# Windowed attention of a hybrid layer rebuilt on half-height tiles, with the values product split around the output projection

## The reference, cut to what matters

```python
def block(i):                                  # for 16 blocks of queries
    q0 = i * Q_BLOCK
    qb = lax.dynamic_slice_in_dim(qg, q0, Q_BLOCK, axis=1)      # 8 heads of 64, 2 kv heads
    kb = lax.dynamic_slice_in_dim(k_pad, q0, band, axis=1)      # band = 384 keys
    vb = lax.dynamic_slice_in_dim(v_pad, q0, band, axis=1)
    valid = ((jnp.abs(k_pos[None, :] - q_pos[:, None]) <= WINDOW)
             & (k_pos[None, :] >= 0) & (k_pos[None, :] < seq_len))
    s_band = jnp.where(valid, einsum(qb, kb) * ATT_SCALE, NEG_INF)
    s_ctx = einsum(qb, kc) * ATT_SCALE                          # 256 context keys
    p = jax.nn.softmax(jnp.concatenate([s_sink, s_ctx, s_band], axis=-1), axis=-1)
    o = einsum(p[..., 1:1 + n_ctx], vc) + einsum(p[..., 1 + n_ctx:], vb)
mix = jnp.concatenate([rms_norm(att, gw[:ATT_W]), rms_norm(hy, gw[ATT_W:])], axis=-1) @ w_out
x = x + g1 * mix
# router: the best of 4 groups, then the best two of its 8 experts
```

## Time and profile before

| | us |
|---|---|
| runs shown, median (lowest to highest) | 2907.66 (2897.3 to 2910.91) |
| the profiled execution | 2909.62 |
| its span, first to last instruction | 2907.9 |
| granted TensorE clock, mean over the span | 0.916 |
| stage 5, first scores to the start of stage 6 | 758.1 |
| PE busy / VectorE / ScalarE / GpSimd over the span | 2491.6 / 1310.2 / 1101.7 / 727.6 |

### The profile page before, as it was taken

One profiled execution on the slowest core, in us unless ns is written; L12 is line 12 of the kernel. 1 busy time (PEld: TensorE's weight loads), 2 busy tenths in 40 slices (PEclk: granted clock), 3 DMA queues, 4 the chain that ended last, 5 costly groups with the idle time before them and its releaser, 6 DMA issues. The chain is left out here.

```text
span 2907.9 us, 45576 instructions
## 1 busy us (share of the span) xinstructions
PE 2491.6 (86%) x15491; PEld 1681.2 (58%) x15492; DVE 1310.2 (45%) x2225; ACT 1101.7 (38%) x2047; POOL 727.6 (25%) x1383
## 2 busy tenths in 40 slices
PE   4887999999959998699999999608888998777997
PEld 1334544444436665589988888505555665544664
DVE  4535473212215554224455444206544665444663
ACT  2542121111124443224454444106444555344562
POOL 1650010000001110512555555531122122221211
PEclk9998999999969998559999999758998999989998
DMA  4983111211173442401111111028876987674893
GB/s 170 314 254 110 31 44 29 73 44 44 29 201 81 118 97 55 120 15 59 59 58 58 58 53 44 30 95 308 283 234 192 348 304 245 225 226 125 297 323 117
DMA packets 238325, 404.73 MB, mean 139 GB/s; under 512 B 24805, under 2 KB 127725, under 8 KB 233413
## 3 DMA queue, kind: packets, MB, share of 16 engines
q1 hardware_dynamic: 160183, 329.28, 33.7%
q0 software_dynamic: 18416, 44.58, 6.6%
q10 hardware_dynamic: 59616, 29.38, 3.7%
HBM read 336.60 MB, written 74.49 MB: 141 GB/s over the span
## 5 line engine op out<-in xcount | busy, mean ns | idle before, releaser
L799 PE MATMUL ps_proj<-sb_hT,sb_win 128*128 128x512 f32 x768 | 336.1, 597 | 7.6 <-DVE sb_rot L904 6.0
L799 PEld LDWEIGHTS ps_proj<-sb_hT,sb_win 128*128 128x128 f32 x768 | 145.7, 192 | 189.9 <-issue 183.0
L2316 PE MATMUL ps_byp<-sb_w,sb_gT 128*128 128x512 f32 x512 | 237.4, 607 | 3.9 <-ACT sb_gT L2131 3.9
L2042 DVE TENSOR_TENSOR sb_w1l<-sb_raw,sb_w1h 128x1024 fp32r<-128x1024 f32 x128 | 148.2, 1220 | 166.3 <-ACT sb_w1h L2103 166.3
L1811 DVE CUSTOM_DVE_ANT_0 sb_pr<-ps_S,sb_mask 128x640 f32<-128x640 f32 x128 | 105.5, 824 | 216.4 <-PE ps_S L1660 216.3
L1346 POOL TENSOR_TENSOR sb_zr<-sb_zr,sb_skip 128x512 f32<-128x512 f32 x32 | 40.0, 1280 | 608.5 <-DMA sb_skip<-in_hy_skip 458.6
L1739 ACT COPY sb_pt<-ps_PT 128x512 f32<-128x512 f32 x128 | 74.7, 584 | 271.4 <-PE ps_PT L1666 271.3
L1680 PE MATMUL ps_O<-sb_v,sb_pt 128*128 128x64 f32 (+1 forms) x1280 | 172.2, 289 | 0.0
L1680 PEld LDWEIGHTS ps_O<-sb_v,sb_pt 128*128 128x128 f32 x1280 | 169.4, 210 | 0.0
L2316 PEld LDWEIGHTS ps_byp<-sb_w,sb_gT 128*128 128x128 f32 x512 | 93.9, 194 | 99.7 <-issue 93.5
L746 PE MATMUL ps_proj<-sb_hT,sb_win 128*128 128x512 f32 x320 | 143.0, 601 | 9.2 <-DMA sb_win<-in_w_in 8.6
(11 more groups left out here) (298 smaller groups left out, 5485.0 us busy)
## 6 DMA issues: line engine op xcount, KB each, us to landing
sb_raw<-in_exp_w SPq DMA_DIRECT2D x64, 2048.0 KB, 15.3
sb_w<-in_exp_w SPq DMA_DIRECT2D x32, 2048.0 KB, 9.9
sb_ada<-in_ada_w SPq DMA_DIRECT2D x16, 1536.0 KB, 8.4
scr_filt<-sb_fout ACTq DMA_DIRECT2D x128, 128.0 KB, 4.4
sb_yh<-scr_filt SPq DMA_DIRECT2D x64, 256.0 KB, 5.0
sb_win<-in_w_in SPq DMA_DIRECT2D x9, 1024.0 KB, 5.6
sb_xr<-in_x SPq DMA_DIRECT2D x16, 512.0 KB, 5.1
sb_gt<-scr_hy_in SPq DMA_DIRECT2D x8, 1024.0 KB, 7.3
```

The lines of the kernel that those rows point to most:

```text
L799: ins = pe.matmul(mp[:, (NQ + n) % 4, :], w[:, pc % 3, k, (ct % 2) * P:(ct % 2 + 1) * P], g.hT[:, k, c * 512:(c + 1) * 512], start=(k == 0 ...
L2042: ve.tensor_tensor(piece(low[m], part), piece(raw13[par][:, m], part), piece(high[m], part).bitcast(F32), ALU.subtract).then_inc(lo[m], 1)
L2316: ins = pe.matmul(yp[:, part, :], gT[:, f, :], w2[par][:, f, part * 512:(part + 1) * 512], start=(f == 0), stop=(f == FT - 1), skip_group_ ...
```

## The change

Scores: the keys of the band lie in rows 0 to 63 of `g.kT`, those of the context in rows 64 to 127, and the queries are loaded into both halves of the rows, so that a head's scores are two products over 64 rows each. The bias row goes; a mask with three variants (first, inner, last tile) takes its place. The heads are taken in the order 0, 4, 1, 5, 2, 6, 3, 7.

Values: the exponentials of all heads are kept (`pt`, one buffer), transposed in ten chunks of four blocks each, ahead of the scores in `head(p)`. Then the values are the weights (64 columns) and two heads at a time stream past them (256 columns), kv head 0 to partitions 0 to 63 of the result and kv head 1 to 64 to 127. The result lies transposed, is copied by ScalarE (`ot`) and turned back by four transposes (`turn_values`). The first half of the product stands between heads 3 and 4, the second between the projection's two halves, the turn after the second half.

Routing: the picks move from GpSimd to VectorE, in three parts behind heads 0, 1 and 2; GpSimd combines them. The inverse roots of the mixer's norm move from VectorE to GpSimd (two operations). On VectorE the normalising moves behind the residual's first half. The router product moves behind head 7. The splitting of `w_out` moves from GpSimd to ScalarE and VectorE, one eighth per head of step 0. All steps are unrolled.

```diff
-    step(Tile(0, -1), True, False, False, False, False)
...
-    with eng.Fori(1, NT // 2 - 1) as j:
-        for off in (1, 2):
-            step(Tile(j, off), True, True, True, True, True)
...
+    for n in range(-1, NT + 3):
+        step(Tile(0, n), n + 1 < NT, 0 <= n < NT, 0 <= n - 1 < NT, 0 <= n - 2 < NT, 0 <= n - 3)
...
+        order = [4 * (p % 2) + p // 2 for p in range(NH)]
+        turns = [(0, 1), (2,), (3,), (4,), (5, 6), (7,), (8,), (9,)]
...
@@ SP
-                    sp.dma_start(qb[b.par][0:HD, :, :], ...)
+                    for part in (slice(0, HD), slice(HD, 2 * HD)):
+                        sp.dma_start(qb[b.par][part, :, :], ...)
...
@@ GpSimd
+                    pool.wait_ge(rt1, pl.n + 1)
...
+                    pool.tensor_tensor(pick[:, b, 2, :], pick[:, b, 0, :], pick[:, b, 1, :], ALU.add).then_inc(picked, 1)
...
+                if values:
+                    pool.wait_ge(sqa, t.n + 1)
...
+                    do(pool.tensor_scalar(nw[:, 1, :], ms[:, t.par, :], 1.0 / HW, EPS, ALU.mult, ALU.add))
+                    rsqrt(nw[:, 0, :], nw[:, 1, :], 2).then_inc(mxr, 1)
@@ TensorE
+                def head(p):
+                    if values:
+                        for c in turns[p]:
+                            pe.wait_ge(ex, 8 * t.n + (4 * c + 3) // 5 + 1)
+                            if c == 1:
+                                wait(pe, att, t.n)
+                            else:
+                                wait(pe, tc, 10 * t.n + (c - 1 if c else 0))
...
+                        pe.matmul(S[:, 512 - C:512], qb[nx.par][HD:2 * HD, h, :], g.kT[HD:2 * HD, kv, 0:C],
+                                  start=True, stop=True)
+                        pe.matmul(S[:, 512:512 + 3 * P], qb[nx.par][0:HD, h, :],
+                                  g.kT[0:HD, kv, bass.ds(nx.n * P, 3 * P)], start=True, stop=True).then_inc(qk, 1)
+
+                def tile_values(half):
+                    pe.wait_ge(tc, 10 * t.n + 5 * half + 5)
+                    if half == 0:
+                        wait(pe, otc, t.n)
                     for a in range(5):
+                        for kv in range(2):
...
+                            ins = pe.matmul(OT[kv * HD:(kv + 1) * HD, half, :, :], v, x, start=(a == 0), stop=(a == 4),
+                                            skip_group_check=True)
                     ins.then_inc(pv, 1)
+                def turn_values():
+                    pe.wait_ge(otc, t.n + 1)
+                    pe.wait_ge(tc, 10 * t.n + 9)
+                    for a in range(4):
+                        ins = pe.transpose(PT[:, t.par, a * P:(a + 1) * P], ot[:, a, :], g.ident[:, :])
+                    ins.then_inc(ott, 1)
...
+                head(7)
                 if route:
...
-                head(7)
-                if values:
-                    head_values(7)
...
                 if project:
                     pe.wait_ge(t1v, pj.n + 1)
+                    project_half(0)
+                if values:
+                    tile_values(1)
+                if project:
+                    project_half(1)
+                if values:
+                    turn_values()
@@ ScalarE
                 head(7)
+                if values:
+                    act.wait_ge(pv, 2 * t.n + 2)
+                    act.copy(ot[:, :, :]..., OT[:, :, :, :]...).then_inc(otc, 1)
@@ VectorE
                 head(0)
                 if route:
                     residual(ro, 1).then_inc(res, 1)
-                for h in range(1, 4):
-                    head(h)
+                if place:
+                    pick_group()
+                head(1)
+                if place:
+                    pick_first()
+                head(2)
+                if place:
+                    pick_second()
+                head(3)
...
                 if values:
                     ve.wait_ge(eso, t.n + 1)
-                    ve.wait_ge(pv, 8 * t.n + 8)
...
+                    ve.wait_ge(ott, t.n + 1)
+                    ve.tensor_tensor(mix..., PT[:, t.par, :]..., rsum..., ALU.mult).then_inc(att, 1)
...
                 if project:
                     do(residual(pj, 0))
+                if values:
+                    ve.wait_ge(mxr, t.n + 1)
+                    wait(ve, t1, t.n)
+                    ve.tensor_scalar(mixn[:, 0, :], mix[t.par][:, 0, :], nw[:, 0, 0:1], None, ALU.mult)
+                    ve.tensor_scalar(mixn[:, 1, :], mix[t.par][:, 1, :], nw[:, 0, 1:2], None, ALU.mult).then_inc(mxn, 1)
```

More of the change, by code:

```diff
@@ L1487, in stage5 @@
         block = st.enter_context(nc.Block())
[L1489 removed]
+        tables = [(mask[:, :, :], i["mask"].rearrange("p (a k) -> p a k", a=3)), (sink[:, :], i["attn_sink"][0].partition_broadcast(P))]
         later = [
@@ new lines, in turn_values, with project_half @@
+                def turn_values():
+                    pe.wait_ge(otc, t.n + 1)
+                    pe.wait_ge(tc, 10 * t.n + 9)
+                    for a in range(4):
+                        ins = pe.transpose(PT[:, t.par, a * P:(a + 1) * P], ot[:, a, :], g.ident[:, :])
+                    ins.then_inc(ott, 1)
+                def project_half(half):
+                    cs = slice(half * 512, (half + 1) * 512)
+                    for k in range(KT):
+                        pe.matmul(M[:, half, :], mixh[:, k, :], woh[:, k, cs], start=(k == 0), stop=False)
+                        pe.matmul(M[:, half, :], mixh[:, k, :], wol[:, k, cs], start=False, stop=False)
+                        ins = pe.matmul(M[:, half, :], mixl[:, k, :], woh[:, k, cs], start=False, stop=(k == KT - 1))
+                    ins.then_inc(op, 1)
@@ L1686, in step @@
+                for p in range(4):
+                    head(p)
                 if route:
@@ new lines, in head @@
+                        ve.wait_ge(sm, 8 * nx.n + p + 1)
+                        ve.tensor_scalar(nm[:, nx.par, p:p + 1], mx[:, nx.par, p:p + 1], -SCALE,
+                                         nsink[:, order[p]:order[p] + 1], ALU.mult, ALU.min).then_inc(nmx, 1)
+                    if values and isinstance(t.n, int) and t.n == 0:
+                        ve.wait_ge(wo_hi, p + 1)
+                        ve.scalar_tensor_tensor(out=wol[:, p, :], in0=wo[:, p, :], scalar=g.cols[:, C_GN + p:C_GN + p + 1],
+                                                in1=woh[:, p, :].bitcast(F32), op0=ALU.mult, op1=ALU.subtract).then_inc(wo_lo, 1)
```

283 lines of the change are left out of this document (121 added, 162 removed).

## The result

The changed kernel takes 3024.75 us (median of 4 runs, 3023.17 to 3033.76) against 2905.81 us for the kernel before (4 runs beside them): 1.0429 times as long, 95% interval 1.0400 to 1.0458. The prediction was 3013, slower with a chance of 0.92. The profiled execution took 3024.8 us with a span of 3023.0.

A forecast was written before the change was run, and what follows sets the result against it. TensorE was taken to set the pace in the middle of the kernel before. Start -29, middle +146 and tail -12 on the profiled 2909.6 us gave 3015, with the median at 3013; range 2965 to 3060.

The forecast's parts named there:

- TensorE's own work: TensorE's work per tile in the loop: 31.2 us against 37, worth 6 us only if TensorE still set the pace.
- The chain: One walk round a loop step, VectorE and TensorE waiting in turn: 45.8 us a tile, 50.3 with the clock's fall.
- C: Loop step, VectorE's masks, residual's second half, picks (5.1) and xn before TensorE can go on with heads: 11.4 us.
- The clock: TensorE's clock falls in each tile during heads 0 to 3: 4.5 us extra a tile, bounds 0 and about 10.
- D: Loop step, TensorE from xn's hand-over through transposes, values and scores until mask 4: 5.4 us, +3 at half speed.
- A: Loop step, TensorE from first projected half to turned values: 13.9 us, +1.5 for the clock at the projection's start.
- The first rival: The clock stays at 1.00 in the loop, 45.8 us a tile: 2951 us; chance 0.15.
- The second rival: Paired passes in scores and values run one after the other, 8 us a tile more: 3117 us; chance 0.05.
- F: Loop step, round trip of head 5 between TensorE's scores and VectorE's mask: 2.1 us.
- G: Loop step, head 7's scores, router, then VectorE's logits, mask 7 and mixl before the projection may start: 6.1 us.
- The tail: End of stage 5: two GpSimd pick chains of 20.1 us replaced, -26; longer steps +12 and +2: -12 us.
- the third rival: VectorE and TensorE overlap as before, a tile of about 34 us: 2813 us; chance 0.08 with near misses.

The follow-up runs named there:

- two runs: Each against the changed kernel: extra TensorE products after heads 0 to 3 and the router, 2986.50 us; router's bias addition moved behind mixl, 2980.24 us.
- The run in one row group: Changed kernel with context scores reading rows 0 to 63 like the band's, so a head's two score products cannot run side by side: 3118.89 us.
- the values first and the picks later: Changed kernel with the values' second half before the projection, the turn between the projection's halves, and picks before the wait for turned values: 2856.41 us.

## Why the prediction was right, and where it was off

- **TensorE's own work.** Right in direction: pairs run side by side, and the values half takes 2.31 us to the next product (forecast 2.26 with one switch). The sum was too low: a step at full clock keeps TensorE busy for 33.2 us and not 31.2, so its list is 4 us a tile shorter and not 6. A part is the pair of scores, 0.84 from its first product to the next operation against 0.75. The miss cost the forecast nothing, since this sum is not on the path. The shorter list was worth nothing in the middle, as forecast, and something in the start.
- **The chain.** Shown: 51.2 a tile against 50.3, and each piece within 0.8 us. Moving the values ahead of the projection gave back 7 us a tile with no work removed. The largest miss is C, 12.2 for 11.4. The picks take 5.9 us, not 5.1: 1.76, 2.42 and 1.73 us in the three gaps, an instruction 0.29 to 0.37 and a last hand-over of 0.3 before the first two masks. Before the third, VectorE waits 0.24 us for its scores, so "heads 1 to 3 wait for VectorE, not for their scores" held for two of the three: at half clock the round trip fills that gap. The middle came to +157 for +146. The first of its steps, which has no picks, is 3.3 us shorter, forecast 4.
- **The clock.** Right in size, 4.4 us a tile by two runs against 4.5, and in place: D and A's start. At full clock D takes 5.46 us, forecast 5.4. The first rival (clock 1.00, 2951 us) did not happen: the clock stood at 0.50 over 17 us in which TensorE was busy 12.5 and no gap was longer than 2.0 us. The Trainium skill (TensorE: Matmul & The Clock Gate, "Why this matters for your kernels") names idle gaps between bursts as what makes the clock fall. The trace goes against using that rule alone.
- **The second rival's price.** Pairs one after the other were to add 1.3 us a tile in scores, in D, F and G. The run in one row group gave 1.4 there, but 1.0 more in C and 1.1 in A.
- **The start.** 102.7 for 105, by steps 22.6, 41.0 and 39.1 for 24, 40 and 40. That GpSimd's work on w_out was not what TensorE waited for is shown for the second step; the third gave 3.7 us.
- **The tail.** Here a step failed: "two pick chains of 20.1 us on GpSimd stand on the path", -26. Only the last does. From the last router product to the prefix product behind it, TensorE in the tail of the changed kernel:

```profile
2031.70 3.60 PE L1697 MATMUL ps_R<-sb_rw,sb_h2T 128*128 128x36 f32 x16 [0.99 <-ACT sb_h2T L1756]
2043.16 0.63 PE L1679 MATMUL ps_R<-sb_pick,sb_upper 128*128 128x32 f32 x2 [7.87 <-POOL sb_pick L1566]
```

and of the kernel before, with the prefix product of the tile ahead, which has no idle time before it:

```profile
1890.99 0.47 PE L1694 MATMUL ps_R<-sb_pick,sb_upper 128*128 128x32 f32 x2
...
1892.88 3.60 PE L1711 MATMUL ps_R<-sb_rw,sb_h2T 128*128 128x36 f32 x16 [0.99 <-ACT sb_h2T L1766]
1921.63 0.64 PE L1694 MATMUL ps_R<-sb_pick,sb_upper 128*128 128x32 f32 x2 [25.16 <-POOL sb_pick L1639]
```

From router to prefix it was 28.7 and is 11.5, -17.3 and once; the tile ahead's prefix product never waited for picks. The other term, +14 for the longer steps, measured +13.4 (from the tail's start to the last router product, 123.6 before and 137.0 after); behind the last prefix product both kernels take 18.1. The forecast "tail under 160" was wrong with it (166.5).
- **The sum.** Stage 5 came to +121.7 for +105: the middle 11 and the tail 8 too low, the start 2 too high. That the time is only 12 above the forecast is in part luck, since stage 6, where nothing was changed, was 6 us shorter in the profiled execution.
- **Faster, 2813 us.** The order of waits excluded it, as argued, and the runs say what it needed: the third rival's condition, a tile under 41.2 us, is met at 39.8 with the values first and the picks later, and the kernel is then faster than before at 2856.

## What to carry to other kernels

Before counting what an edit saves on the busiest engine, walk once round the step and ask of each engine whose turn it is: a product moved to "between" two others can make a second engine stand through both, and a shorter instruction list is then worth nothing. Where an order is written by hand, put the work that feeds the other engine's long list first, and the other engine's free work (here the picks) into what waits remain. When a tail or start has several chains, look at the end of each for an idle row before taking its length off.

## What was not expected of the hardware

- Extra products can make a kernel faster: 32 more of 256 columns a step after the heads, and eight after the router, raised the clock from 0.80 to 0.97 and took 3.3 us off a tile. In the idle stretch before xn alone, eight of them (1.2 us) brought 0.95 to 0.99 and took 1.3 us off a tile; after each of heads 0 to 3 and after the router, in the same order, they gave back what they won.
- With the clock at half in part of the steps, their lengths can differ although their work is equal. With the values first and the picks later they are 38.2, 39.9 and 41.5 us in turn (the last 40.9); so a single step is not to be read for all in such a kernel.
- Two score products on different row groups start within 10 ns of each other. The pass of 256 columns shows 0.48 us beside the other as it does alone; the first pass of 384 shows 0.59, and 0.48 alone. Both products together take 0.91 us from the first's start to the last's end at full clock, and 1.34 in one row group.
